# Hymba step on one Trainium2 core: output gates by Sigmoid on ScalarE, head norm weights as the scale of the copies of the transposed rows

## The reference, cut to what matters

```python
def rms_norm(x, g):
    x32 = x.astype(jnp.float32)
    return x32 * lax.rsqrt(jnp.mean(x32 * x32, axis=-1, keepdims=True) + EPS) * g.astype(jnp.float32)

def mixer_output(h_m, mo, a, g_m, g_da, lam_init, w_out, dtype):
    B, T = mo.shape[0], mo.shape[1]
    hm = rms_norm(h_m, g_m).transpose(0, 2, 1, 3).reshape(B, T, H_M * D_V_M) * jax.nn.sigmoid(mo.astype(jnp.float32))
    ha = (rms_norm(a, g_da) * (1.0 - lam_init)).transpose(0, 2, 1, 3).reshape(B, T, H_DA * D_V_DA)
    return jnp.concatenate([hm, ha], axis=-1).astype(dtype) @ w_out
```

## Time and profile before

| | us |
|---|---|
| median of 3 runs | 664.82 |
| lowest, highest | 664.41, 667.9 |
| the profiled execution, its own time | 669.12 |
| its span | 667.4 |
| PE busy in the span | 603.3 (90%) |
| PE weight loads busy | 330.7 (50%) |
| VectorE busy | 282.7 (42%) |
| ScalarE busy | 141.0 (21%) |
| GpSimd busy | 118.2 (18%) |

### The profile page before, as it was taken

The page is one execution under the profiler, slowest core; times in us unless marked ns, Lnnn a source line. Parts: engine busy times, 40 slices in busy tenths (PEclk is TensorE's granted clock), DMA queues, the critical chain, the costliest instruction groups (busy, mean ns, idle before and its releaser), DMA issues.

```text
span 667.4 us, 9139 instructions
## 1 busy us (share of the span) xinstructions
PE 603.3 (90%) x3405; PEld 330.7 (50%) x3405; DVE 282.7 (42%) x644; ACT 141.0 (21%) x424; POOL 118.2 (18%) x205
## 2 busy tenths in 40 slices
PE   4999999899899999999979974999999996999692
PEld 2544544345555554555535563655555553555331
DVE  2320068433234457478686667423221311112067
ACT  3110151234332554321032010101010010101012
POOL 2341016220021010101032101012312110210013
PEclk9999999899899999999989985999999997999897
DMA  9635246932412120008759796999999999999983
GB/s 297 209 112 178 77 149 195 291 121 94 162 51 77 47 82 0 2 2 234 217 235 402 239 368 219 380 416 420 403 417 419 419 421 421 423 419 421 417 345 136
DMA packets 59486, 165.72 MB, mean 248 GB/s; under 512 B 18389, under 2 KB 27958, under 8 KB 46770
## 3 DMA queue, kind: packets, MB, share of 16 engines
q1 hardware_dynamic: 49666, 147.90, 58.1%
q0 software_dynamic: 7552, 17.19, 8.0%
q10 hardware_dynamic: 2224, 0.04, 0.2%
HBM read 150.88 MB, written 23.21 MB: 261 GB/s over the span
## 4 chain that ended last, share of the span: by engine, by line
PE 69%; DMA 15%; DVE 7%; ACT 4%; issue 2%; POOL 2%; SPq 0%; POOLq 0%; DVEq 0%; ACTq 0%
PE bank L2101 13%; PE bank L2323 8%; PE bank_p L2375 8%; PE bank L2098 8%; PE scores L2392 8%; PE bank_t L2375 6%; DMA WS<-in_w_down_e 5%; DMA XHT<-in_w_down_e 5%; DMA MO<-in_cache_k,pages 2%; PE bank L2365 2%; DMA WS<-in_w_in 2%; PE bank_p L2226 2%; PE scores L2243 1%; PE scores L2194 1%; PE bank_t L2346 1%
## 5 line engine op out<-in xcount | busy, mean ns | idle before, releaser
L2101 PE MATMUL bank<-WS,XHT 128*128 128x512 f32 x192 | 89.9, 616 | 2.4 <-DMA WS<-in_w_in 1.9
L2098 PE MATMUL bank<-XHT,WS 128*128 128x512 f32 x192 | 86.7, 607 | 0.6 <-PE bank_t L2117 0.6
L2098 PEld LDWEIGHTS bank<-XHT,WS 128*128 128x128 f32 x192 | 36.3, 193 | 43.8 <-issue 43.5
L2101 PEld LDWEIGHTS bank<-WS,XHT 128*128 128x128 f32 x192 | 36.0, 196 | 44.4 <-issue 41.8
L2375 PE MATMUL bank_p<-WS,XHT 128*64 128x256 f32 x256 | 43.3, 381 | 2.1 <-DMA XHT<-in_w_up_e 1.3
L1008 POOL DMA_INDIRECT out_rows<-MVA,slot_ids x15 | 15.1, 1009 | 153.3 <-DVE MVA L1895 150.6
L2375 PE MATMUL bank_t<-WS,XHT 128*64 128x256 f32 x224 | 39.4, 381 | 0.2 <-DVE XHT L1878 0.2
L896 POOL TENSOR_SCALAR rr<-ss 128x1 f32<-128x1 f32 (+3 forms) x25 | 8.4, 337 | 145.8 <-ACT DVt L1284 41.3
L2375 PEld LDWEIGHTS bank_p<-WS,XHT 128*64 128x64 f32 x256 | 26.8, 137 | 14.4 <-DMA XHT<-in_w_up_e 1.7
L1895 DVE COPY MVA<-scores 128x512 f32<-128x512 f32 x16 | 11.1, 692 | 51.1 <-PE scores L2392 51.1
L2392 PE MATMUL scores<-WS,FT 128*64 128x512 f32 x72 | 27.2, 648 | 5.4 <-DMA WS<-in_w_down_e 5.4
(11 more groups left out here) (481 smaller groups left out, 1048.6 us busy)
## 6 DMA issues: line engine op xcount, KB each, us to landing
WS<-in_w_gate_e SPq DMA_DIRECT2D x16, 1024.0 KB, 24.1
WS<-in_w_up_e SPq DMA_DIRECT2D x14, 1024.0 KB, 20.3
WS<-in_w_down_e SPq DMA_DIRECT2D x14, 1024.0 KB, 28.8
WS<-in_w_in SPq DMA_DIRECT2D x6, 2048.0 KB, 10.8
XHT<-in_w_up_e SPq DMA_DIRECT2D x10, 1024.0 KB, 22.4
XHT<-in_w_down_e SPq DMA_DIRECT2D x9, 1024.0 KB, 27.9
XHT<-in_w_gate_e SPq DMA_DIRECT2D x8, 1024.0 KB, 28.6
FT<-in_w_up_e SPq DMA_DIRECT2D x6, 1024.0 KB, 22.1
```

Source lines behind the costliest of these rows:

```text
L2098: mm = pe.matmul(PS[r][:, :], w[:, k, 128 * m:128 * (m + 1)], hT[:, k, 0:512], start=(k == 0), stop=(k == KC - 1))
L2101: mm = pe.matmul(PS[r][:, :], hT[:, k, 128 * m:128 * (m + 1)], w[:, k, :], start=(k == 0), stop=(k == KC - 1))
```

## The change

- ScalarE evacuates the gate products by a plain copy. Five new instructions, ("sig", j) for a whole tile of 512 columns, apply Sigmoid in place, all in one batch after ("mdec1"), in the order T4, 0, 1, 2, 3. The thirty VectorE instructions of the old gates are gone.
- The multiplications by head norm weights are gone from VectorE (L1477 with the gates, L1683 in "ona"). The weight is instead the per-partition scale of the copy by which ScalarE takes the transposed rows out of PSUM: there a partition is a feature of a head.
- VectorE's last multiplication of "on" waits for the gate of its tile (mo_gated).
- The two loads of the weights bring 128 x 1 values in place of 128 x 128, and the final state gets a tile of its own.
- SP's move of the decode gates stands later, with the new items.

The diff, cut to its core:

```diff
+GATED = (T4, 0, 1, 2, 3)
...
-    gates_of = lambda j: [("sig", j, 0), ("sig", j, 1)]
-    order += gates_of(0) + [("decay", 0)] + more() + [("tp",) + prev, ("mqk_s", 0)] + gates_of(1) + more()
+    order += [("decay", 0)] + more() + [("tp",) + prev, ("mqk_s", 0)] + more()
...
-    order += norm("oa") + [("sig", 2, 0)] + more() + [("mpa", 1)] + gates_of(T4) + more() + [("mqk_s", 2), ("sig", 2, 1)] + more()
-    order += [("mpb", 1), ("decay", 3), ("mdec1",)] + more() + [("mpa", 2), ("sig", 3, 0)] + more() + [("mqk_s", 3)] + more()
-    order += [("mdecq", 0), ("mpb", 2)] + more() + [("mdecq", 1), ("mpa", 3)] + more() + [("sig", 3, 1), ("mpb", 3), ("wsk",)] + more()
+    order += norm("oa") + more() + [("mpa", 1)] + more() + [("mqk_s", 2)] + more()
+    order += [("mpb", 1), ("decay", 3), ("mdec1",)] + [("sig", j) for j in GATED] + more() + [("mpa", 2)] + more() + [("mqk_s", 3)] + more()
+    order += [("mdecq", 0), ("mpb", 2)] + more() + [("mdecq", 1), ("mpa", 3)] + more() + [("mpb", 3), ("wsk",)] + more()
...
-                     (gm[:, :], head_norm_m[0].partition_broadcast(128)),
+                     (gm, head_norm_m[0].rearrange("(d a) -> d a", a=1)),
...
-            def turned_rows(dst, src, j):
+            def turned_rows(dst, src, j, gain):
                 src = src.rearrange("p (k t) -> p k t", t=128)
                 if j < NT:
-                    return copy(dst[:, 0:4, col(j):col(j) + 128], src)
+                    return copy(dst[:, 0:4, col(j):col(j) + 128], src, gain)
...
-                        ins = act.activation(MO[:, m, :], src[:, :], ACT.Exp, scale=-1.0)
+                        ins = copy(MO[:, m, :], src[:, :])
...
+                elif kind == "sig":
+                    j = item[1]
+                    n = nrows(j)
+                    drained(act, ("acc", "mo", j) if j < NT else ("small", "mo"), "a%d" % (j % 2) if j < NT else small_bank("mo"))
+                    act.activation(MO[0:n, j, :], MO[0:n, j, :], ACT.Sigmoid).then_inc(mo_gated, 1)
...
-                    link(v.tensor_scalar(mo, mo, 1.0, None, ALU.add))
-                    link(v.reciprocal(mo, mo))
-                    mo = mo.rearrange("p (h d) -> p h d", d=DV)
-                    link(v.tensor_tensor(mo, mo, gm[0:n, None, :].to_broadcast([n, 2, DV]), ALU.mult))
...
                     if att:
-                        v.tensor_tensor(hd, hd, gda[0:n, None, :].to_broadcast([n, 4, DV]), ALU.mult).then_inc(ho_ready, 1)
+                        ins.then_inc(ho_ready, 1)
                     else:
+                        link(ins)
+                        dve.wait_ge(mo_gated, GATED.index(j) + 1)
                         if j == T4:
                             dve.wait_ge(dm_out, 16 * 6)
                         v.tensor_tensor(ho, ho, MO[0:n, j, :], ALU.mult).then_inc(ho_ready, 1)
```

More of the change, by code:

```diff
@@ L282, in build @@
         maskneg = sb("maskneg", [128, 128])
-        head_gains = sb("head_gains", [128, 2, DV])
-        gm, gda = head_gains[:, 0, :], head_gains[:, 1, :]
+        final_C = sb("final_C", [128, H * DQ])
+        head_gain = sb("head_gain", [128, 2])
+        gm, gda = head_gain[:, 0:1], head_gain[:, 1:2]
         gmix, gffn = sb("gmix", [128, KC]), sb("gffn", [128, KC])
@@ L677, in _ @@
                         sp.dma_start(MVA[S0:N4, T4, :, 0:DV], MVA[SX:NX, T4, :, 0:DV]).then_inc(dm_out, 16)
-                elif item == ("sig", T4, 1):
+                elif item == ("sig", T4):
                     sp.wait_ge(mo_gated, 1)
@@ L1098, in copy @@
                 return act.activation(dst, src, ACT.Copy, scale=scale)
-            def turned_rows(dst, src, j):
+            def turned_rows(dst, src, j, gain):
                 src = src.rearrange("p (k t) -> p k t", t=128)
                 if j < NT:
-                    return copy(dst[:, 0:4, col(j):col(j) + 128], src)
-                copy(dst[:, 0:4, col(j):col(j) + NMETA], src[:, :, 0:NMETA])
-                return copy(dst[:, 0:4, col(j) + SX:col(j) + NX], src[:, :, S0:N4])
+                    return copy(dst[:, 0:4, col(j):col(j) + 128], src, gain)
+                copy(dst[:, 0:4, col(j):col(j) + NMETA], src[:, :, 0:NMETA], gain)
+                return copy(dst[:, 0:4, col(j) + SX:col(j) + NX], src[:, :, S0:N4], gain)
             for item in ORDER:
@@ L1174, in _ @@
                         else:
-                            ins = act.activation(MO[0:NX, T4, cols], src, ACT.Exp, scale=-1.0)
+                            ins = copy(MO[0:NX, T4, cols], src)
                     ins.then_inc(freed[r], 1)
@@ L1289, in _ @@
                     after(act, item, "t")
-                    ins = turned_rows(dqT, PS["t"][:, :], j)
+                    ins = turned_rows(dqT, PS["t"][:, :], j, gda)
                     ins.then_inc(freed["t"], 1)
@@ L1294, in _ @@
                     after(act, item, "Sa")
-                    ins = turned_rows(hT, Sps[:, 0, 0:512], j)
+                    ins = turned_rows(hT, Sps[:, 0, 0:512], j, gm)
                     ins.then_inc(freed["Sa"], 1)
@@ L1467, in decode_state @@
                     v.nop().then_inc(wsk_ready, 1)
-                else:
-                    j, half = item[1:]
-                    n = nrows(j)
-                    drained(dve, ("acc", "mo", j) if j < NT else ("small", "mo"), "a%d" % (j % 2) if j < NT else small_bank("mo"))
-                    mo = MO[0:n, j, 256 * half:256 * half + 256]
-                    link(v.tensor_scalar(mo, mo, 1.0, None, ALU.add))
-                    link(v.reciprocal(mo, mo))
-                    mo = mo.rearrange("p (h d) -> p h d", d=DV)
-                    link(v.tensor_tensor(mo, mo, gm[0:n, None, :].to_broadcast([n, 2, DV]), ALU.mult))
-                    if item == ("sig", T4, 1):
-                        v.nop().then_inc(mo_gated, 1)
             def mask_products(b, m, dst):
@@ L1670, in _ @@
                             link(ins)
-                elif kind in ("mdec1", "mdecq", "mdec2", "mdec3", "wsk", "sig"):
+                elif kind in ("mdec1", "mdecq", "mdec2", "mdec3", "wsk"):
                     decode_state(kind, item)
@@ L1679, in _ @@
                     hd = ho.rearrange("p (u d) -> p u d", d=DV)
-                    link(v.tensor_tensor(hd, hd, rr8[0:n, j, slice(4, 8) if att else slice(0, 4), None].to_broadcast([n, 4, DV]),
-                                         ALU.mult))
+                    ins = v.tensor_tensor(hd, hd, rr8[0:n, j, slice(4, 8) if att else slice(0, 4), None].to_broadcast([n, 4, DV]),
+                                          ALU.mult)
                     if att:
-                        v.tensor_tensor(hd, hd, gda[0:n, None, :].to_broadcast([n, 4, DV]), ALU.mult).then_inc(ho_ready, 1)
+                        ins.then_inc(ho_ready, 1)
                     else:
+                        link(ins)
+                        dve.wait_ge(mo_gated, GATED.index(j) + 1)
                         if j == T4:
```

6 lines of the change are left out of this document (3 added, 3 removed).

## The result

The changed kernel took **657.29 us** (median of 9 runs, 654.57 to 661.76), the kernel before 664.41, timed beside it (9 runs, 662.96 to 668.91): ratio 0.9884, 95% interval 0.9859 to 0.9909. The forecast was 662.1 with a range down to 659.7. Ratios and differences of means use the fast runs alone and leave out those that the record calls slow.

What follows compares the result with a forecast made beforehand. The expert weight stream, started by PE's chain before 410 us, was taken to set the end. Terms 1.62 + 0.7 - 0.12 + 0.56 = 2.76 us off the median 664.82 gave 662.1 us, range 659.7 to 666.1.

Steps and rivals of the forecast that it cites:

- What bounds the kernel, and that a gain before 410 us arrives whole: Expert weight stream sets the end and hangs on PE's chain until 410 us; mixer gains before then arrive one to one.
- the gain doesn't arrive: Rival: the change works only beside other work and the weight stream ends as before; 664.8 us, chance 0.18.
- Gate group, 1.62: Fourth head: without the tenth gate group ahead of it, VectorE's division starts 1.62 us earlier, shortening PE's wait before transposes.
- Attention weight, 0.7: Attention norm: one of five weight products leaving VectorE ends a PE wait, gaining 0.7 us; the others nothing.
- Pointer scale, -0.12: ScalarE's copy of transposed rows: a pointer scale costs 0.12 us more where PE waits for the copy.
- Sigmoids, table loads, nine groups: nothing: Sigmoids and first load fit ScalarE's idle time, second load hides behind VectorE's placing, nine gate groups behind PE's products: zero.
- DMAs: nothing: Norm weight loads as 128 x 1 and the later move of decode gates on SP: no effect on time.
- What is late next is VectorE's own queue: After the gate group goes, VectorE's division, five key products, projection sums and norm are late next; 0.6 of PE's wait stays.
- The clock, 0.56: Dip behind the waits at 340 and 345 us: 2.31 us lost before, 1.75 stays, gaining 0.56; bounds zero and 2.31.
- the clock stays up: Rival: no dip remains after the transposes, so 2.31 replaces 0.56; gain 4.5, 660.3 us, chance 0.25.
- The clock comes up late: Rival: first expert turn's up products run at low clock, costing 2.86 us; 665.5 us if the dip stays, chance 0.12.

Runs made afterwards that it cites:

- b_last_group: Kernel before, with only the tenth gate group moved from ahead of the fourth head's division to the ninth's place; ratio 0.9973.
- a_wsk_late: Changed kernel with VectorE's product of the state's keys moved from ahead of the first normed rows to behind the third; ratio 0.9947 to the kernel before.
- a_sig_late: Changed kernel with the sigmoid batch listed behind the fourth head; PE, VectorE, ScalarE and GpSimd orders stayed the same; ratio 0.9906 to the kernel before.
- after_fourth: Changed kernel timed again without any edit, in a later group of runs; ratio 0.9911 to the kernel before.
- b_two_waits: Kernel before, with the tenth gate group moved next to the ninth and head norm weights as scale of the copies; no Sigmoid; ratio 0.9928.
- b_two_waits_again: Same kernel as b_two_waits, timed again in another group beside after_fourth; ratio 0.9955 to the kernel before.
- a_ona_product: Changed kernel with the attention norm's second product put back on VectorE, multiplying by ones; ratio 0.9973 to the kernel before.
- after_again: Changed kernel timed again without any edit, in a later group of runs; ratio 0.9879 to the kernel before.
- a_fill_short: Changed kernel with two unread dummy products put on PE ahead of the second mLSTM transposes; ratio 0.9893 to the kernel before.
- b_fill_short: Kernel before, with two unread dummy products put on PE ahead of each of the first two mLSTM transposes; ratio 0.9976.

## Why the prediction was wrong

- **What bounds the kernel, and that a gain before 410 us arrives whole:** right. 12.13 us ahead at the gather, 11.85 at the end. The rival "the gain doesn't arrive" falls.
- **Gate group, 1.62:** right. b_last_group gives 1.62 alone; in the changed kernel it is 1.82. Of the 0.2 more the traces show only that VectorE's evacuation behind the key products follows them at once, where it had idled 0.52 before.
- **Attention weight, 0.7:** right, 0.73 in every execution without the product.
- **Pointer scale, -0.12:** -0.09. The pair at one shape that the earlier trace rows lacked is in the changed kernel: 682 ns with the pointer, 597 without. The 93 ns of the Trainium skill, "ScalarE: Activation LUTs", section "What ACT_TABLE_LOAD costs", is nearer than the 117 that I took from unlike shapes.
- **Sigmoids, table loads, nine groups: nothing:** right as far as PE's waits show. Sigmoids 612 ns against the estimate of 600, the batch over at 304.10. Both new loads took 1283 ns beside idle time, and the work behind each began within 0.02 us; the 2.7 us per switch of that page's "Rules for kernel authors" appears nowhere. The second load ends at 393.99, while VectorE's placing of the later rows, for which the first gate products wait, runs on to 399.98.
- **DMAs: nothing:** not borne out, as far as 18 profiles tell. The gather of the first routed rows is about 1.1 us shorter in those with the 128 x 1 weights and what goes with them, and PE waits for it. The prediction looked at the loads that the edit moves, and not at this one.
- **"What is late next is VectorE's own queue":** half right. The chain now runs by ScalarE's squares and GpSimd's roots (1.20 us) to VectorE, and a_wsk_late shows that clearing VectorE's queue brings little.
- **The clock, 0.56: this is the step that failed.** I had set the loss before at 2.31 and let 1.75 of it stay, by the dip of the earlier trace rows. Measured, PE lost 2.76: the transposes 0.46, near my 0.45, and the 16 products 9.16 - 6.87 = 2.29, where I had 1.86, because twice the 3.65 of eight products is 7.30 and not the 6.87 that sixteen take at full clock. In the five profiles of the changed kernel (a_sig_late among them) it lost nothing twice and 1.7 three times (one of the three is after_fourth's, of an execution of 672.84 us); b_two_waits, b_two_waits_again and a_ona_product, with the same two waits of 0.40 and 2.28, lost nothing twice and 1.7 once. So the dip that I kept is real and of the right size, but it comes in some executions and not in others: the term is 2.76 or 1.07, in the mean of the five 1.75, and neither is 0.56.
- **What that makes of the sum:** with the mean of 1.75 the stage gives 0.73 - 0.09 + 1.82 + 1.75 = 4.2 us, and with the gather's 1.1 it is 5.3; the later groups have 4.8. The dip of the earlier trace rows, from which I took the 1.75, stands behind one wait of 1.96; none of the five profiles with 0.83 to 1.49 us at that point shows a dip there. The rival "the clock stays up" had the mechanism, for about half of the executions, and its 660.3 was the nearest of the times named. The rule of the Trainium skill that I cited with it ("TensorE: Matmul & The Clock Gate", section "HAM oscillation — how this bites in real kernels") held in direction: less idle time, fewer dips. That short gaps cost nothing did not hold: waits of 0.40 and 2.28 us are followed by a low clock in four of those eight profiles.
- **The range** failed by a second omission. I read the clock in one stage only. From 10 to 300 us the clock also dips (at 128, 170, 205 or 290 us), in some executions and not in others, at a cost of about 1.6 to 3.3 us each, with the same instructions; at 128 and 205 us waits of PE of up to 2.0 us come and go as well. One profile against a median of three runs left 4.3 us unexplained in the prediction, and I gave that scatter no width. The 2 to 3 us by which the first comparison's gain exceeds that of the later groups aren't accounted for by any mechanism shown here.
- **"The clock comes up late":** no. The first gate products took 6.56 us at the low clock, the up products 3.63 at the full one, as in the earlier trace rows.

## What to carry over

Where PE waits twice within a few microseconds, price the waits and the granted clock behind them as one thing: here 2.55 us of removed waiting brought 1.1 or 2.8 more by the clock, by execution. When a clock term hangs on a dip, count in how many executions it occurs before choosing one value, look at whether the wait ahead of it is there in each, and lay two traces beside each other product by product, to see how much of their difference lies in code that nobody edited. To take an instruction out of a queue pays only to the next releaser: here GpSimd's roots, 0.4 us on.

## What was not expected of the hardware

- Identical code meets different clocks. after_again's trace is level with that of the changed kernel up to 160 us and 2.7 us behind it at 208: 1.6 by a low clock at 170 us, behind the same waits of 0.43 and 0.56 us in both, and 1.1 at 205 us, where PE waits 0.90 us for VectorE (L1632) in one and not in the other. At 170 us all 18 profiles have these two waits, and 12 have the low clock.
- Part of what looks like scatter of the clock is scatter of PE's waits. At 205 us nine of the 18 profiles have a wait of about 1.6 us, and seven of these a low clock behind it; of the nine with 0.9 us or less, none has one.
- Products of no use can keep the clock up: two of 0.9 us in each of two waits took 2.4 ± 0.7 us off what the clock costs in a run. In the traces the ones that fitted the waits brought 2.5 and 2.6 us at this place (a_fill_short, b_fill_short), though b_fill_short's ratio as a whole, 0.9976, is not clear of no change; four in each gave back no more than they cost (1.0012).
- A Sigmoid of 128 x 512 takes 612 ns, a plain copy of that shape 597, a copy with a pointer scale 682.
